# Expert results weighted at eviction and added to the residual rows in DRAM by the scatter

## The reference

```python
def hier_moe(x, w_group, w_router, w_gate, w_up, w_down):       # 4 groups x 8 experts, FF 512
    g_sel = argmax(x @ w_group);  g_w = softmax(x @ w_group)[g_sel]
    e_top, e_idx = top_k(logits of the 8 experts of g_sel, 2)
    weight = softmax(e_top) * g_w                               # two weights per token
    # for each token and each of its two experts e:
    y = (silu(h @ w_gate[e]) * (h @ w_up[e])) @ w_down[e]
    return sum over the two of weight * y

h = rms_norm(x, ffn_norm[i]);  x = x + hier_moe(h, ...)         # in both layers
```

## Time and profile before

| | us |
|---|---|
| median of three runs | 1803.39 (1800.02 to 1805.4) |
| the profiled execution | 1801.87 |
| its span | 1800.0 |
| TensorE matmuls busy | 1620.6 (90%) |
| VectorE / ScalarE / GpSimd busy | 434.9 / 425.0 / 200.5 |
| moved by DMA | 468.10 MB, mean 260 GB/s |

### The profile page before, as it was taken

How to read it: one execution, slowest core, us unless ns; L and a number is a source line. 1 busy time by engine, 2 the same in 40 slices (tenths; PEclk the granted TensorE clock), 3 DMA queues, 4 the chain that set the end, 5 groups by cost and what they waited for, 6 DMA issues and landing times.

```text
span 1800.0 us, 22070 instructions
## 1 busy us (share of the span) xinstructions
PE 1620.6 (90%) x7890; PEld 775.3 (43%) x7890; DVE 434.9 (24%) x1104; ACT 425.0 (24%) x930; POOL 200.5 (11%) x288
## 2 busy tenths in 40 slices
PE   6995889979999999999499989899799999999993
PEld 3544566533333333333246457664433333333331
DVE  1475832430000000000312235442610000000002
ACT  2443272311111111111100246651211111111110
POOL 2240220000000000000201013220000000000000
PEclk9997989989999999999699989889999999999997
DMA  7210126259999999999705020014399999999993
GB/s 233 73 68 6 47 63 261 70 231 404 421 422 421 422 421 422 422 422 377 193 8 184 36 62 1 0 78 202 127 373 422 421 421 422 422 422 422 422 406 151
DMA packets 110909, 468.10 MB, mean 260 GB/s; under 512 B 34105, under 2 KB 40505, under 8 KB 61708
## 3 DMA queue, kind: packets, MB, share of 16 engines
q1 hardware_dynamic: 103564, 450.67, 62.7%
q0 software_dynamic: 5120, 8.41, 1.2%
q10 hardware_dynamic: 2176, 8.39, 1.2%
HBM read 456.91 MB, written 18.91 MB: 264 GB/s over the span
## 4 chain that ended last, share of the span: by engine, by line
PE 81%; DVE 10%; issue 3%; ACT 3%; DMA 2%; POOL 1%; DVEq 0%; ACTq 0%; SPq 0%; POOLq 0%
PE bank L1697 24%; PE bank L1710 13%; PE bank L1677 10%; PE bank L1316 8%; PE bank L504 6%; PE bank L374 3%; PE bank L399 3%; PE bank L1687 2%; PE bank L742 2%; PE bank L386 2%; DVE arena L1096 2%; PE bank L1703 2%; DVE arena L1792 2%; DVE m L1095 2%; DMA arena<-y_d 1%
## 5 line engine op out<-in xcount | busy, mean ns | idle before, releaser
L1697 PE MATMUL bank<-arena 128*64 128x512 f32 x2048 | 450.6, 592 | 1.4 <-ACT arena L1691 1.4
L1697 PEld LDWEIGHTS bank<-arena 128*64 128x64 f32 x2048 | 149.1, 137 | 290.8 <-issue 289.0
L1710 PE MATMUL bank<-arena 128*64 128x512 f32 x1024 | 233.8, 598 | 35.2 <-DVE arena L1792 35.2
L1788 DVE TENSOR_TENSOR arena<-arena,bank 128x256 f32<-128x256 f32 x64 | 26.9, 421 | 664.5 <-ACT arena L1778 664.5
L1716 POOL DMA_INDIRECT y_d<-arena,slot_row x64 | 62.6, 978 | 947.6 <-ACT arena L1783 947.6
L1677 PE MATMUL bank<-arena 128*64 128x512 bf16 x1152 | 154.2, 396 | 8.2 <-DVE arena L1670 8.2
L1316 PE MATMUL bank<-arena 128*128 128x512 f32 x320 | 140.3, 601 | 0.8 <-issue 0.8
L1710 PEld LDWEIGHTS bank<-arena 128*64 128x64 f32 x1024 | 68.8, 136 | 156.3 <-issue 129.9
L1778 ACT ACTIVATE arena<-bank 128x256 f32<-128x256 f32 x64 | 24.5, 384 | 400.5 <-PE bank L1697 400.5
L504 PE MATMUL bank<-arena 128*128 128x512 f32 x256 | 111.2, 593 | 1.7 <-ACT arena L313 1.7
L742 PE MATMUL bank<-arena 128*128 128x512 f32 (+1 forms) x288 | 106.8, 532 | 0.0
(11 more groups left out here) (281 smaller groups left out, 1487.2 us busy)
## 6 DMA issues: line engine op xcount, KB each, us to landing
arena<-in_moe_w_gate SPq DMA_DIRECT2D x64, 2048.0 KB, 14.2
arena<-in_moe_w_up SPq DMA_DIRECT2D x64, 2048.0 KB, 18.9
arena<-in_moe_w_down SPq DMA_DIRECT2D x64, 2048.0 KB, 16.6
arena<-in_even_w_in SPq DMA_DIRECT2D x4, 2048.0 KB, 8.5
arena<-y_d ACTq DMA_DIRECT2D x8, 1024.0 KB, 8.4
arena<-bias_row_d SPq DMA_DIRECT2D x2, 3584.0 KB, 11.8
arena<-in_odd_w_in SPq DMA_DIRECT2D x3, 2048.0 KB, 7.8
arena<-in_even_w_out SPq DMA_DIRECT2D x2, 2048.0 KB, 7.9
```

The source lines that it names most:

```text
L1697: mm = nc.tensor.matmul(bank[1][fh * CAP:(fh + 1) * CAP, :], xeT[:, j, half * CAP:(half + 1) * CAP], wgu[u][:, :, n, fh * FH:(fh + 1) * FH ...
L1710: mm = nc.tensor.matmul(bank[3][dh * CAP:(dh + 1) * CAP, :], hidT[:, j, fh * CAP:(fh + 1) * CAP], wd[u][:, n, dh * 512:(dh + 1) * 512], st ...
```

## The change

- The scatter no longer writes to a buffer of results but adds to rows of x in DRAM (`x_rows`): 1024 rows of 512 floats, for layer one a buffer `x_d`, for layer two the output itself.
- So x must lie there before. SyncE stores `xt` in two halves, when the mixer's additions of each half are done (`store_x`), and GpSimd's first scatter waits for both stores.
- The weights are applied when ScalarE copies the result out of its bank (`y_out`, operand `slot_w`). They reach the slots as the row numbers do: `row_w` holds row number and weight beside each other, `named` gets a second plane, and TensorE's product of names has 64 columns instead of 32. ScalarE's first `y_out` waits for the table.
- After the loop there are no adds. In layer one ScalarE reads x back, 512 KB per tile, and the norm follows. After layer two nothing is read or stored; SyncE waits for the last scatter. `odd_sp` waits for the fence where it waited for the adds.
- The gather's third pass moves behind `hid_turn` (`pick_begin`, `pick_end`).

```diff
@@ -211,7 +211,7 @@
-        y_d = [dram(f"y_d{n}", [2 * NA, 512]) for n in range(2)]
+        x_rows = [dram("x_d", [2 * SEQ, 512]), out[0].rearrange("t (h c) -> (t h) c", h=2)]
@@ -1280,7 +1281,7 @@
         def odd_sp(sp):
-            sp.wait_ge(S("m_x"), 2 * NT)
+            fence(sp, "m", 0)
@@ -1393,7 +1394,7 @@
-            norm_act(act, "n2", lambda e, i: e.wait_ge(S("m_x"), 2 * i + 2))
+            norm_act(act, "n2", lambda e, i: e.wait_ge(S(f"m_xin{i}"), 16))
@@ -1714,8 +1714,14 @@
         def scatter_y(t, layer, u, n):
             return nc.gpsimd.indirect_dma_start(
-                out=y_d[layer][:, :], out_offset=bass.IndirectOffsetOnAxis(ap=slot_row[:, n:n + 1], axis=0),
-                in_=yb[:, u, :], in_offset=None, bounds_check=2 * NA - 1, oob_is_err=False).then_inc(S(f"{t}_yout"), 16)
+                out=x_rows[layer], out_offset=bass.IndirectOffsetOnAxis(ap=slot_row[:, n:n + 1], axis=0),
+                in_=yb[:, u, :], in_offset=None, bounds_check=2 * SEQ - 1, oob_is_err=False,
+                compute_op=ALU.add).then_inc(S(f"{t}_yout"), 16)
+
+        def store_x(sp, t, layer, half):
+            sp.dma_start(x_rows[layer].rearrange("(i p h) c -> p i h c", p=P, h=2)[:, :, half, :],
+                         xt[:, :, half * 512:(half + 1) * 512]).then_inc(S(f"{t}_xout"), 16)
@@ -1737,10 +1743,17 @@
-        def picked(pe, t, c):
+        def pick_begin(pe, t, c):
             pe.wait_ge(S(f"{t}_ones"), c + 1)
             pe.wait_ge(S(f"{t}_rows"), c + 1)
-            pick_rows().then_inc(S(f"{t}_picked"), 1)
+            pick_rows(range(2))
+
+        def pick_end(pe, t, c):
+            pick_rows(range(2, 3)).then_inc(S(f"{t}_picked"), 1)
...
@@ -1777,10 +1790,11 @@
-            nc.scalar.activation(yb[:, u, :], bank[3][:, :], ACT.Copy).then_inc(S(f"{t}_y"), 1)
+            nc.scalar.activation(yb[:, u, :], bank[3][:, :], ACT.Copy,
+                                 scale=slot_w[:, bass.ds(e, 1)]).then_inc(S(f"{t}_y"), 1)
@@ -1847,7 +1861,9 @@
-            sp.wait_ge(S(f"{mixed}_add"), past(f"{mixed}_add") + 2 * NT)
+            for half in range(2):
+                sp.wait_ge(S(f"{mixed}_add"), past(f"{mixed}_add") + (half + 1) * NT)
+                store_x(sp, t, L, half)
             one_weight(sp, t, L, 2, 2, 0)
@@ -1919,8 +1935,10 @@
                 if after >= 2:
-                    picked(pe, t, c + 2)
+                    pick_begin(pe, t, c + 2)
                 hid_turn(pe, t, c)
+                if after >= 2:
+                    pick_end(pe, t, c + 2)
                 down(pe, t, c, cu, u)
@@ -1976,17 +1996,19 @@
-            for i in range(NT):
-                act.dma_start(y_rows[:, :, i, :], y_d[L].rearrange("(t k h) c -> t k (h c)", k=2, h=2)[i * P:(i + 1) * P]).then_inc(S(f"{t}_yin{i}"), 16)
+            if L == 0:
+                for i in range(NT):
+                    act.dma_start(xt[:, i, :], x_rows[L].rearrange("(t h) c -> t (h c)", h=2)[i * P:(i + 1) * P]).then_inc(S(f"{t}_xin{i}"), 16)
...
-            pool.wait_ge(S(f"{t}_slot_rows"), L + 1)
+            pool.wait_ge(S(f"{t}_slot_rows"), 2 * (L + 1))
+            pool.wait_ge(S(f"{t}_xout"), 32 * (L + 1))
@@ -2086,7 +2110,8 @@
+            v_.tensor_copy(slot_w[:, 0:NE], bank[5][:, NE:2 * NE]).then_inc(S(f"{t}_slot_rows"), 1)
@@ -2120,16 +2146,9 @@
-            for i in range(NT):
-                dve.wait_ge(S(f"{t}_yin{i}"), 16 * (L + 1))
-                for k in range(2):
-                    v_.scalar_tensor_tensor(xt[:, i, :], y_rows[:, k, i, :], weight[:, k, i:i + 1], xt[:, i, :],
-                                            ALU.mult, ALU.add).then_inc(S(f"{t}_x"), 1)
...
             if L == 0:
-                norm_row(dve, "n2", NT - 1)
+                for i in range(NT):
+                    norm_row(dve, "n2", i)
@@ -2140,10 +2159,8 @@
-            for i in range(NT):
-                sp.wait_ge(S("m_x"), 2 * NT + 2 * i + 2)
-                sp.dma_start(out[0, i * P:(i + 1) * P, :], xt[:, i, :]).then_inc(S("out"), 16)
-            sp.wait_ge(S("out"), 16 * NT)
+            sp.wait_ge(S("m_xout"), 64)
+            fence(sp, "m", 1)
```

More of the change, by code:

```diff
@@ L229, in build @@
         slots = sb("slots", [P, CAP])
-        y_row = sb("y_row", [P, 2, NT])
+        row_w = sb("row_w", [P, 2, NT, 2])
         half_row = sb("half_row", [P, 1])
         slot_row = sb("slot_row", [P, NE + 1], I32)
+        slot_w = sb("slot_w", [P, NE + 1])
         gain = sb("gain", [P, DM])
@@ L1019, in even_pool @@
             c(g_.iota(slots[:], [[1, CAP]], base=-AWAY, channel_multiplier=0, allow_small_or_imprecise_dtypes=True))
[L1020 removed]
+            c(g_.iota(row_w[:, :, :, 0], [[0, 2], [2 * P, NT]], base=1, channel_multiplier=2, allow_small_or_imprecise_dtypes=True))
             c(g_.iota(half_row[:], [[1, 1]], base=0, channel_multiplier=1, allow_small_or_imprecise_dtypes=True))
@@ L1593, in build @@
                             o_work, odd_weigh, odd_finish, before=even_att)
-        weight = sb("weight", [P, 2, NT])
+        weight = row_w[:].rearrange("p k i w -> p w k i")[:, 1]
         more_i = sb("more_i", [P, 1 + NX], I32)
@@ L1638, in build @@
         is_slot = at(r0, 2 * NT, 2, CAP); r0 += 2 * NT * P
-        named = at(r0, 2 * NT, NE); r0 += 2 * NT * NE
+        named = at(r0, 2 * NT, 2, NE); r0 += 2 * NT * 2 * NE
         row_f = at(r0, NE); r0 += NE
@@ L1671, in pick_ones, with pick_rows @@
                                            slots[:].unsqueeze(1).broadcast_to((P, NT, CAP)), ALU.is_equal)
-        def pick_rows():
-            for part in range(3):
+        def pick_rows(passes=range(3)):
+            for part in passes:
                 for i in range(NT):
@@ L1738, in ones_for, with picked @@
             pick_ones(e).then_inc(S(f"{t}_ones"), 1)
-        def picked(pe, t, c):
+        def pick_begin(pe, t, c):
             pe.wait_ge(S(f"{t}_ones"), c + 1)
             pe.wait_ge(S(f"{t}_rows"), c + 1)
-            pick_rows().then_inc(S(f"{t}_picked"), 1)
+            pick_rows(range(2))
+        def pick_end(pe, t, c):
+            pick_rows(range(2, 3)).then_inc(S(f"{t}_picked"), 1)
+        def picked(pe, t, c):
+            pick_begin(pe, t, c)
+            pick_end(pe, t, c)
         def rows_out(act, t, c):
@@ L1909, in slot_names @@
                 for n in range(2 * NT):
-                    mm = nc.tensor.matmul(bank[5][:, 0:NE], flat(is_slot[:, n]), named[:, n, :],
+                    mm = nc.tensor.matmul(bank[5][:, 0:2 * NE], flat(is_slot[:, n]), flat(named[:, n]),
                                           start=(n == 0), stop=(n == 2 * NT - 1))
@@ L1930, in more @@
                 for n in range(2 * NT):
-                    mm = nc.tensor.matmul(bank[5][:, 0:1], flat(x_slot[:, n]), y_row[:, n // NT, n % NT:n % NT + 1],
+                    mm = nc.tensor.matmul(bank[5][:, 0:2], flat(x_slot[:, n]), row_w[:, n // NT, n % NT, :],
                                           start=(n == 0), stop=(n == 2 * NT - 1))
@@ L1967, in body @@
                     rows_out(act, t, c + 2)
-                y_out(act, t, c, u)
+                if isinstance(c, int) and c == L * NE:
+                    act.wait_ge(S(f"{t}_slot_rows"), 2 * (L + 1))
+                y_out(act, t, c, u, e)
             per_expert(act, L, body)
@@ L2079, in moe_dve @@
             link(v_.tensor_tensor(dest_f[:], base, xbase, ALU.add))
-            link.loose(v_.tensor_tensor(named, ohf, flat(y_row[:]).unsqueeze(2).broadcast_to((P, 2 * NT, NE)), ALU.mult))
+            for w in range(2):
+                link.loose(v_.tensor_tensor(named[:, :, w, :], ohf, row_w[:].rearrange("p k i w -> p w (k i)")[:, w].unsqueeze(2).broadcast_to((P, 2 * NT, NE)),
+                                            ALU.mult))
             for r in range(2):
@@ L2088, in moe_dve @@
                           (S(f"{t}_slots"), L + 1)).then_inc(S(f"{t}_slot_rows"), 1)
-            dve.wait_ge(S(f"{t}_slot_rows"), L + 1)
+            v_.tensor_copy(slot_w[:, 0:NE], bank[5][:, NE:2 * NE]).then_inc(S(f"{t}_slot_rows"), 1)
+            dve.wait_ge(S(f"{t}_slot_rows"), 2 * (L + 1))
             link(v_.tensor_tensor(cmpx, xend.unsqueeze(1).broadcast_to((P, NX, NE)), iota32[:, 0:NX].unsqueeze(2).broadcast_to((P, NX, NE)), ALU.is_le))
@@ L2106, in more @@
                 dve.wait_ge(S(f"{x}_step"), j * X_STEPS + 1)
-                more_link.enter(j, 5)
+                more_link.enter(j, 6)
                 for r in range(2):
@@ L2114, in more @@
                 x_step(dve, x, j, X_PICKED)
+                more_link.loose(v_.tensor_copy(slot_w[:, NE:NE + 1], bank[5][:, 1:2]))
                 rows_of_slots(dve, more_link, slot_row[:, NE:NE + 1], bank[5][:, 0:1], x_row_f, x_no_row,
```

8 lines of the change are left out of this document (2 added, 6 removed).

## The result

The changed kernel takes 1790.55 us (median of seven runs, 1788.18 to 1795.22) against 1802.89 us (1800.02 to 1805.6, also seven runs) of the kernel before: a ratio of 0.9934, with a 95% interval from 0.992 to 0.9947. It is 12 us faster, inside the range given, and less than half of the 25 us forecast. The profiled executions have spans of 1800.0 and 1790.3 us.

The account below looks back on a forecast made before the run. The expert loops were taken as bound by TensorE (14.89 us per expert) and DMA (15.29), close together. Tail -20.1, layer change -8 and loops +3 made -25.1 against 1801.87, with 1.5 to the median: 1777 us, range 1757 to 1800.

Parts of the forecast that it names:

- The loops: Both expert loops: with DMA as the limit each changes by 28x - 9.7 us; +3 us together at x = 0.4.
- x: Expert loops: DMA time per expert that the adding scatter takes beyond the plain one's 0.345 us; taken as 0.4 us.
- gate-up waiting from the middle of a layer on: Expert loops, sign of being wrong: gate-up matmuls waiting for weights that early would mean x is larger.
- The layer change: Last scatter of layer one to layer two's projection: no adds, half the bytes read; gain 5.2 to 10.2 us, taken as 8.
- the lead of 9.7 us: Expert loops: how much shorter a layer's loop can get before it waits for weights, 9.6 to 9.9 us.
- a last read over 13 us after the first: Layer change, sign of being wrong: the last read landing over 13 us after the first is issued.
- The tail: After layer two's last scatter: output already in DRAM when it lands, no adds, reads or stores; -20.1 us.
- the term of 0 for those edits: Ahead of the first expert: the larger table of slots costs 0, give or take 0.5 us per layer.
- (a): Expert loops: adding scatter nearly free to the engines, x below 0.2; 1754 us at x = 0; chance 0.13.
- (b): Expert loops: adding scatter costs two to three plain ones, x 0.6 to 0.85; 1788 to 1802 us; chance 0.10.
- (c): Expert loops: adding scatters stop weight loads behind them, x from 0.85, slower; counter-argument: plain scatters cost loads' time per byte; chance 0.14.
- (d): Expert loops: moved pass brings nothing as DMA is the limit already; loops give 56x alone, 1796 us; chance 0.03.

Follow-up runs that it names:

- e7: The changed kernel, with layer two loading only half of each expert's down weights, third pass moved: 1767.45 us, ratio 0.9804 to the kernel before.
- e8: The changed kernel with layer two loading half of each expert's down weights and the gather's third pass in its old place: 1790.78 us, ratio 0.993.
- e1: The kernel before, with only the gather's third pass moved behind the turn of the hidden rows: 1787.28 us, ratio 0.991.
- e4: The changed kernel, with SyncE issuing layer two's compression weights only after ScalarE's four reads of x have landed: 1782.54 us, ratio 0.9888 to the kernel before.
- e5: The changed kernel, but layer one scatters plainly, reads back and adds as before the change; third pass moved in both layers: 1786.44 us, ratio 0.9916.
- e6: The changed kernel with the third pass in its old place and the compression weights issued after the reads of x: 1788.73 us, ratio 0.9921.
- e3: The changed kernel, but layer two's scatter writes its rows without adding them: 1780.07 us, ratio 0.9867 to the kernel before.

## Why the prediction was right and wrong

**The loops: right.** Forecast 2 (28x - 9.7) with x = 0.4, so +1.5 each; measured +2.4 and +2.8, of which 1.7 each are the clock. The value x is 0.40 and 0.43 by the pace of the landings, and 0.41 by the records of the scatters' queue. The estimate by the Trainium skill's passage on ReduceScatter (Collectives: The Full Stack), a halved rate and x = 0.345, was close and a little low: this case's add takes 2.2 times the plain scatter's engine time (0.76 against 0.35 us). The records show twice the packets at 1.1 times the time each; how much of that is the second read, they don't show. TensorE's side was too low: the move saves 0.67 us per expert where it is free to (e7, e8), not 0.57, which costs the forecast nothing, as DMA sets the end. Of the loops' signs all but one came as written: I had gate-up waiting from the middle of a layer on as a sign of a larger x. It waited from 671 us on, the 21st of 32 experts, with x as forecast, and it had to: at the sixth expert the lead is 9.7 + 26 * 0.4 = 20 us, it goes at 0.4 + 0.67 + 0.4, about 1.45 us per expert, and 14 experts later it is gone. That sign was badly worked out.

**The clock in the loops: missed.** I had the last experts wait for weights and gave the wait no price beyond itself. The last gate-up took 1.7 us more in each layer.

**The layer change: the step that failed, in size.** Forecast -8, measured 30.07 to 28.52, -1.55; the landing under load and the contended reads took the rest. The terms: I had the reads start 3.7 us after the last scatter; it was 7.2, so 3.5 lost. Of the landing's 7.0 us, 2.7 were there before, 3.6 come with engines that are still full (e1 has 6.3 with a plain scatter) and 0.7 with the add, for which I had 0.8. Then I took a value between free and contended reads; the contended end it was, which is 2.8 more. Both were in the text in another place: I had used up the lead of 9.7 us in the loop, but not asked who else lived on it. The uncontended reads of e4 took 7.9 us from the first issue to the last landing, where I had 8.1. The sign of being wrong that I had set here, a last read over 13 us after the first, came with 13.6.

**The tail: a second step too cheap.** Forecast -20.1, measured -15.4. The landing took 4.2 us, not 3.4, and the last waits 4.3, not 0.3, so that the span ends 8.5 us after the last scatter starts and not "some 4": GpSimd's closing DRAIN. Before the change it ran from 1779.92 to 1785.29, beside the reads and VectorE's adds; now it is at the end. This is the cover that I should have named.

**The rest.** 2.7 us of the profiled difference lie ahead of the first expert; they are within what this stretch does by itself (e5 has 371.6 there, e6 377.0), and e1, which has none of the edits to the routing, has the same 376.4. So the term of 0 for those edits is neither borne out nor contradicted. Sum of the misses: 2.2 in the loops, 6.5, 4.7, 2.7, and -0.7 in the second mixer, 15.4 together; -25.1 + 15.4 = -9.7, the difference of the spans. The medians are 12 apart.

**The rivals.** (a), (b) and (c) fall with x between 0.40 and 0.43; that loads keep their 2.4 us per MB speaks against (c) too. The argument against (c) was misread, though: 2.3% for 2.56 MB is 2.7 us of the engines per MB, so a plain scatter costs about an eighth more per byte than loads do, not the same. (d), the moved pass brings nothing, had 0.03 and was named for the wrong reason: alone the move brings 17 us. But in the company of the add it brings nothing that shows, and the loops still don't cost 56x, because without the move the same lead is there to pay for the add. Move and add draw on one account: by the stages the move alone is worth 15.4 us, the add with all that it does away with 11.7, and both together 11.7 (17, 17 and 12 in the medians).

**Open.** What decides that the clock falls after the last wait: it did after 2.75 and 2.86 us in two places and not after 2.74, 2.78 and 2.80 in three others; it did after each of 3.3 us and more, and after none of 2.54 or less. And why GpSimd's DRAIN takes 5.37 us in the four kernels with a plain scatter in a layer, the one before, e1, e3 and e5, and 2.9 in the six whose scatters all add. In e5 the plain scatters are in layer one alone, some 900 us ahead of it, so it is not the last scatter that decides. Neither was tried by itself.

## What to carry to other kernels

When a loop's loads run ahead of its matmuls, find out how long the lead is, and list all that live on it: the next stage's weights, the last scatter, the first reads. Two edits that each use the lead up don't add; measure them apart before adding them. And of a tail that is cut off, ask what other engines still have to do after it: the closing work that was hidden beside it becomes the end.

## What the runs showed of the hardware

- An indirect scatter that adds takes 2.2 times the DMA engine time of a plain one for the same bytes: 0.76 against 0.35 us of the 16 engines for 128 KB, data packets of 2048 bytes and 176 ns against 4096 bytes and 159 ns.
- Its instruction takes 1.55 us on GpSimd instead of 0.97. It lands 4.2 to 4.6 us after its issue with the engines empty (plain: 2.6) and 7.0 to 7.2 behind other loads (plain: 5.9 to 6.3).
- GpSimd's DRAIN at the end of the program took 5.4 us in the four kernels that have a plain scatter anywhere and 2.9 us in the six whose scatters all add.
- TensorE's granted clock dropped to its lower level after a single wait in a loop that was otherwise dense, and cost the next 32 matmuls 1.7 us: after all six waits of 3.3 to 3.4 us, two of five of 2.74 to 2.86 us, and none of 2.54 us or less.
